# Two heads' pairs of scores ahead and one pair of values behind in three attentions, and four modulation slabs in another place

## The reference

```python
# first block
mod = silu(c) @ w_ada + b_ada                        # "ada1": 6 x 1024 columns
h = rms_norm(x, g1) * (1 + scale1) + shift1
# 8 heads of 64 ("na"): softmax(q k / 8 + bias table) v ; 8 heads of 96 ("mla"): softmax(q k / sqrt(96)) v
merged = sigmoid(gate_na) * (y_na @ w_proj_na) + sigmoid(gate_mla) * (y_mla @ w_proj_mla)
x = x + gate1 * (merged @ w_out)
h2 = rms_norm(x, g2) * (1 + scale2) + shift2         # "the second norm"
x = x + gate2 * (routed_experts(h2) + shared_expert(h2))   # 64 experts, 8 for each token
# second part: two layers; each has its modulation ("ada2": 2 x 3 x 1024 columns)
shift, scale, gate = split(silu(c) @ ada_w[layer] + ada_b[layer])
# layer 0: spatial gating and Fourier mixing on x and on 256 context tokens ("ab")
# layer 1: 16 heads of 64 ("c"), one softmax over [sink, 256 context keys, 256 windowed keys]
out = rms_norm(x, final_g)
```

## Time and profile before

| what | value |
|---|---|
| median of 3 runs | 1321.85 us (1320.67 to 1326.89) |
| the profiled execution | 1322.2 us, its span 1320.4 us |
| TensorE busy | 1255.9 us, 95% of the span |
| VectorE, ScalarE, GpSimd busy | 35%, 25%, 4% |
| mean DMA rate | 251 GB/s over the span |
| mean granted TensorE clock | 0.987 |

### The profile page before, as it was taken

One profiled execution on the slowest core, in us unless ns is written; L12 is line 12 of the kernel. 1 busy time (PEld: TensorE's weight loads), 2 busy tenths in 40 slices (PEclk: granted clock), 3 DMA queues, 4 the chain that ended last, 5 costly groups with the idle time before them and its releaser, 6 DMA issues.

```text
span 1320.4 us, 19746 instructions
## 1 busy us (share of the span) xinstructions
PE 1255.9 (95%) x7605; PEld 776.5 (59%) x7640; DVE 464.1 (35%) x1291; ACT 326.9 (25%) x672; POOL 47.1 (4%) x71
## 2 busy tenths in 40 slices
PE   5999998898899999999999999999999999999886
PEld 3787675587544444444444444446845558888455
DVE  1109594333633333333333333333300112330852
ACT  1213413403222222222222222222211111211761
POOL 0001001111000000000000000000000001000001
PEclk8899999999999999999999999999999999999998
DMA  9936699934399999999999999996121110240000
GB/s 386 345 128 247 267 364 404 376 121 186 125 392 389 387 390 387 388 389 387 388 382 383 383 385 387 389 387 262 64 68 59 64 64 33 96 139 21 1 1 32
DMA packets 47806, 331.61 MB, mean 251 GB/s; under 512 B 5232, under 2 KB 7376, under 8 KB 7824
## 3 DMA queue, kind: packets, MB, share of 16 engines
q1 hardware_dynamic: 44640, 325.08, 62.2%
q10 hardware_dynamic: 2896, 4.19, 0.9%
q0 software_dynamic: 224, 1.70, 0.3%
HBM read 329.90 MB, written 1.05 MB: 251 GB/s over the span
## 4 chain that ended last, share of the span: by engine, by line
PE 91%; ACT 3%; DMA 3%; DVE 2%; issue 1%; SPq 0%; ACTq 0%; DVEq 0%
PE bank L669 18%; PE bank L394 12%; PE bank L693 9%; PE bank L755 8%; PE bank L641 7%; PE bank L649 6%; PE bank L813 4%; PE bank L381 3%; PE bank L317 3%; PE bank L581 2%; PE bank L852 2%; PE bank L567 2%; DMA ring<-stream 2%; PE bank L460 2%; ACT pT L1106 2%; PE bank L371 2%
## 5 line engine op out<-in xcount | busy, mean ns | idle before, releaser
L669 PE MATMUL bank<-ring,arena 128*64 128x512 f32 x1088 | 240.7, 594 | 0.4 <-DMA ring<-experts 0.3
L394 PE MATMUL bank<-hT,ring 128*128 128x256 f32 x736 | 166.1, 386 | 7.2 <-ACT arena L1146 4.1
L394 PEld LDWEIGHTS bank<-hT,ring 128*128 128x128 f32 x736 | 141.7, 194 | 30.9 <-issue 11.3
L669 PEld LDWEIGHTS bank<-ring,arena 128*64 128x64 f32 x1088 | 76.1, 137 | 136.0 <-issue 136.0
L693 PE MATMUL bank<-ring,arena 128*64 128x512 f32 x544 | 124.2, 598 | 0.0
L641 PEld LDWEIGHTS bank<-arena 128*128 128x128 bf16 x1680 | 95.3, 98 | 28.3 <-issue 28.3
L641 PE MATMUL bank<-arena 128*128 128x128 bf16 x1680 | 105.4, 219 | 0.2 <-DVE arena L1630 0.2
L755 PE MATMUL bank<-hT,ring 128*128 128x512 f32 x240 | 104.6, 592 | 0.0
L649 PE MATMUL bank<-arena 128*128 128x512 bf16 x363 | 83.7, 379 | 1.7
L1155 ACT COPY arena<-bank 128x512 f32<-128x512 f32 x70 | 41.0, 586 | 168.6 <-PE bank L641 168.6
L1662 DVE TENSOR_TENSOR arena<-bank,arena 128x512 f32<-128x512 f32 x68 | 43.8, 686 | 105.5 <-ACT arena L1164 105.5
(11 more groups left out here) (296 smaller groups left out, 1349.2 us busy)
## 6 DMA issues: line engine op xcount, KB each, us to landing
ring<-experts SPq DMA_DIRECT2D x204, 1024.0 KB, 7.8
ring<-stream SPq DMA_DIRECT2D x105, 1024.0 KB, 7.0
arena<-consts POOLq DMA_DIRECT2D x1, 1408.0 KB, 7.9
resid<-x SPq DMA_DIRECT2D x1, 1024.0 KB, 6.0
resid<-ctx ACTq DMA_DIRECT2D x1, 1024.0 KB, 5.8
out<-arena ACTq DMA_DIRECT2D x8, 128.0 KB, 2.1
arena<-rpb ACTq DMA_DIRECT2D x2, 438.0 KB, 22.2
cs<-consts ACTq DMA_DIRECT2D x1, 432.5 KB, 9.3
```

Of the source, the lines that this page charges most:

```text
L394: mm = mmul(o[:, 0:n_tok], w[:, k, t * P:(t + 1) * P], hT[:, k, 0:n_tok], start=(k == 0), stop=(k == KT - 1))
L669: mm = mmul(bank[B_GU][64 * u:64 * u + 64, :], xg[:, kk, SLOTS * u:SLOTS * u + SLOTS], w[u][:, k, :], start=(kk == 0), stop=(kk == KT - 1))
```

## The change

Scores run two pairs ahead. "na" and "mla" become one sequence of eight pairs (`EARLY`), so "mla" scores start while "na" still runs. `values` of pair p-1 come after `turn` of pair p. The pairs' scores alternate between banks 0, 1 and 5, 7; outputs have bank 4 alone; in "c" the turned groups go round banks 2, 3 and 5, and the turned probabilities have four buffers (two of them in the arena). The ada2 slabs are split anew: four ahead of the first `turn` (behind `ada_fold(1)`), two with each of the eight pairs, and four in the gap of the second norm, one before its sum and three after. `ada_fold(3)` and `ada(3)` move to the end of "ab", `ada_quarters(3)` behind the router's sigmoid. `pn` no longer waits for "mla"; `wo` waits for `merged` tile by tile; the context's sum takes bank 7, `rtT` bank 4, and `shu` banks 6 and 7.

```diff
+        def turned_at(kind, h):
+            if kind == "c":
+                return pT[:, h % 2, :] if h % 4 < 2 else ar((8192, 13632)[h % 2], 1024)
+            return pT[:, h % 2, 512 * (h % 4 // 2):512 * (h % 4 // 2) + 512]
-        FILL = {(kind, i): [("ada2", 3 * (4 * n + i) + j) for j in range(3)]
-                for n, kind in enumerate(("na", "mla")) for i in range(4)}
+        EARLY = [("na", i) for i in range(4)] + [("mla", i) for i in range(4)]
+        FIRST_FILL = [("ada2", j) for j in range(4)]
+        FILL = [[("ada2", 4 + 2 * p + j) for j in range(2)] for p in range(8)]
+        LAST_FILL = [("ada2", j) for j in range(20, 24)]
...
-                                    open_group(name, h % 2)
+                                    open_group(name, ((0, 1), (5, 7))[i % 2][h % 2])
...
-                        o = open_group(name, 2 + (h % 2 if per == 1 else j))
+                        o = open_group(name, 2 + h % 2 if per == 1 else (2, 3, 5)[(2 * h + j) % 3])
...
-                    o = open_group(name, 4 + i % 2)
+                    o = open_group(name, 4)
...
+            def early_attention():
...
                 scores(0)
+                scores(1)
+                ada_fold(1)
+                for f in FIRST_FILL:
+                    ada_slab(*f)
+                for p, (kind, i) in enumerate(EARLY):
+                    if p + 2 < len(EARLY):
+                        scores(p + 2)
+                    ops[kind][1](2 * i)
+                    ops[kind][1](2 * i + 1)
+                    for f in FILL[p]:
                         ada_slab(*f)
+                    if p >= 1:
+                        values(p - 1)
+                values(7)
+                ada_fold(2)
+
+            def last_attention():
+
+                scores, turn, values = pair_of_heads("c")
+                scores(0)
+                scores(1)
+                for i in range(8):
+                    if i < 6:
+                        scores(i + 2)
                     turn(2 * i)
                     turn(2 * i + 1)
-                    values(i)
+                    if i >= 1:
+                        values(i - 1)
+                values(7)
...
-            pe.wait_ge(S("merged"), 8)
...
+                        if d == 0:
+                            pe.wait_ge(S("merged"), k + 1)
...
+            ada_slab(*LAST_FILL[0])
             two_sums("sq2", "sum2", 0)
+            for f in LAST_FILL[1:]:
+                ada_slab(*f)
...
-            t_tiles("shu", ("shu", 0), 2, [0, 5], 256)
+            t_tiles("shu", ("shu", 0), 2, [6, 7], 256)
...
+            exponents(*EARLY[0])
+            exponents(*EARLY[1])
+            for p in range(8):
+                turned(*EARLY[p])
+                if p < 6:
+                    exponents(*EARLY[p + 2])
+                if p == 3:
+                    ada_quarters(2)
...
+            maxima(0)
+            maxima(1)
+            for p, (kind, i) in enumerate(EARLY):
+                for h in (2 * i, 2 * i + 1):
...
+                    normalise(kind, h, 256)
+                if p >= 2:
+                    rows_out(p - 2)
+                if p + 2 < len(EARLY):
+                    maxima(p + 2)
+                if p == 0:
+                    ada(1)
+            rows_out(6)
+            rows_out(7)
+            ada(2)
...
-            c_scores(0)
-            c_scores(1)
+            for h in range(4):
+                c_scores(h)
             for i in range(8):
...
-                if i < 7:
-                    c_scores(2 * i + 2)
-                    c_scores(2 * i + 3)
-                if i >= 1:
-                    c_out(i - 1)
+                if i >= 2:
+                    c_out(i - 2)
+                if i < 6:
+                    c_scores(2 * i + 4)
+                    c_scores(2 * i + 5)
+            c_out(6)
             c_out(7)
```

More of the change, by code:

```diff
@@ L459, in values, with scores @@
                             hd = head(h)
-                            mm = mmul(o[hd["o"]:hd["o"] + 64, 0:256], hd["v"](kt), pT[:, h % 2, 256 * kt:256 * kt + 256],
+                            mm = mmul(o[hd["o"]:hd["o"] + 64, 0:256], hd["v"](kt), turned_at(kind, h)[:, 256 * kt:256 * kt + 256],
                                       start=(kt == 0), stop=(kt == 2 * per - 1))
                     close_group(mm, name)
-                scores(0)
[L465 to L470, removed]
-                        ada_slab(*f)
+                return scores, turn, values
+            def early_attention():
+                ops = dict(na=pair_of_heads("na"), mla=pair_of_heads("mla"))
+                def scores(p):
+                    kind, i = EARLY[p]
+                    ops[kind][0](i)
+                def values(p):
+                    kind, i = EARLY[p]
+                    ops[kind][2](i)
+                scores(0)
+                scores(1)
[8 more added lines that the diff above has]
+                    for f in FILL[p]:
+                        ada_slab(*f)
+                    if p >= 1:
[9 more added lines that the diff above has]
+                        scores(i + 2)
                     turn(2 * i)
                     turn(2 * i + 1)
-                    values(i)
+                    if i >= 1:
+                        values(i - 1)
+                values(7)
             pe.wait_ge(S("ones_set"), 1)
@@ L552, in _ @@
             pe.wait_ge(S("qk_ready"), 8)
-            attention("na")
-            attention("mla")
-            ada_fold(3)
+            early_attention()
             done(pe, ("na", "o", 3))
-            done(pe, ("mla", "o", 3))
             for half in range(2):
@@ L565, in _ @@
                         o = open_group((tag, d), b + 2 * (d % 2))
+                        if tag == "pm" and d == 0:
+                            done(pe, ("mla", "o", 2))
+                            done(pe, ("mla", "o", 3))
                         for k in range(4):
@@ L798, in _ @@
                     over_chunk(i - 9)
+            ada_fold(3)
             oab = []
@@ L842, in _ @@
                 done(pe, ("v2", t))
-            attention("c")
+            last_attention()
             done(pe, ("c", "o", 7))
@@ L1108, in _, with exponents @@
-            attention("na")
-            attention("mla")
+            def exponents(kind, i):
+                nk = KINDS[kind][2]
+                for h in (2 * i, 2 * i + 1):
+                    act.wait_ge(S(kind + "_negmax"), h + 1)
+                    if kind == "c":
+                        a.activation(att[:, h % 4, 6:8], att[:, h % 4, 2:4], ACT.Exp, bias=vv("sink", h, h + 1))
+                    if kind == "mla":
+                        full(act, ("na", "t", h + 4, 0) if h < 4 else ("mla", "t", h - 4, 0))
+                    for t in range(TT):
+                        o = probs(kind, h)[:, nk * t:nk * t + nk]
+                        src = bk((kind, "s", h))[:, 256 * t:256 * t + 256] if kind == "mla" else o
+                        ins = a.activation(o, src, ACT.Exp, bias=att[:, h % 4, 2 + t:3 + t],
+                                           scale=96 ** -0.5 if kind == "mla" else 1.0,
+                                           accum_out=att[:, h % 4, 4 + t:5 + t])
+                    if kind == "mla":
+                        emptied(ins, (kind, "s", h))
+                    else:
+                        ins.then_inc(S(kind + "_exp"), 1)
@@ new lines, in turned @@
+            def turned(kind, i):
+                for h in (2 * i, 2 * i + 1):
+                    for j in range(KINDS[kind][2] // 256):
+                        full(act, (kind, "t", h, j))
+                        emptied(a.copy(turned_at(kind, h)[:, 512 * j:512 * j + 512], bk((kind, "t", h, j))[:, :]), (kind, "t", h, j))
+            exponents(*EARLY[0])
[6 more added lines that the diff above has]
+                    ada_quarters(2)
@@ L1137, in _ @@
             emptied(a.activation(small[:, 0:128], bk("rt")[:, 0:128], ACT.Sigmoid), "rt")
+            ada_quarters(3)
             second_part(0)
@@ L1247, in _ @@
                     emptied(a.activation(g2s[:, 2 * s + t, :], bk((f"g2{s}", t))[:, 0:256], ACT.Silu), (f"g2{s}", t))
-            attention("c")
+            exponents("c", 0)
+            exponents("c", 1)
+            for i in range(8):
+                turned("c", i)
+                if i < 6:
+                    exponents("c", i + 2)
             load_table(ACT.Sqrt)
```

72 lines of the change are left out of this document (16 added, 56 removed).

## The result

The changed kernel takes 1303.76 us (median of 4, 1302.35 to 1304.08) against 1323.88 us for the kernel before on the same chip (1320.67 to 1326.89): a ratio of 0.9834, 95% interval 0.9813 to 0.9854, so it is faster, by 1.7%. The forecast was 1302.4 us. The profiled execution took 1303.9 us with a span of 1302.1 us, 18.3 us less than the one before. The medians are 20.1 us apart, since the executions of the kernel before lie in two groups (1320.7 and 1321.9 us, 1325.9 and 1326.9 us) and the profiled one belongs to the first. It is the pair of profiled executions that the table divides.

What follows compares the result with a forecast made beforehand. TensorE, 91% of the chain, was taken as the bound. Gains of 9.8 - 0.5 + 1.4 + 0.4 + 3.4 + 4.9 = 19.4 us off 1322.2, less 0.35 for the median, gave 1302.4 us; range 1297.5 to 1307.

Steps and rivals of the forecast that it cites:

- Forecast 9.8: First attentions: the fold after them ends at 246.2 us against the merge's start at 256.03, a gain of 9.8 us.
- The pause before the first fold: First attentions: TensorE stands about 3.4 us for bank 7 until VectorE has added head 3's bias.
- rival (1): Clock falls in the pause before the first fold: 1.8 us, 1304.2; with a second fall around `pos` 1306; chance 0.22.
- the sum of TensorE's own work: First attentions from 202.9 us: turnings, slabs, `values`, scores and one bank wait add to 42.7 us, ending at 245.6.
- rival (2): DMA bounds the first attentions; if all four slabs' gain of 3.7 us were lost, 1306.1 us; chance 0.05.
- one of the signs I had named for a wrong prediction: Gap before the router: the prediction is wrong if the router starts later after the norm because of the three slabs.
- The term that I had put at 3.4: Shared expert: with banks 6 and 7 VectorE reads `pos` at 343.9 instead of 347.34 us; bounds 2.0 and 4.1.
- the allowance of 0.33 us in each of seven pairs: Last attention: small waits traded between TensorE and VectorE move its end from 1273.5 to 1275.8 us; gain 4.9.
- Rival (3): VectorE holds the last attention at nearly 7 us a pair; that part gives 1.7 us, total 1305.6; chance 0.10.
- rival (4): Slower: transposes behind the next pair's maxima lengthen each of 16 pairs; 1.3 us each eats the gain; chance 0.02.
- the other sign that I had named for a wrong prediction: Expert stage: it only shifts as a whole; the prediction is wrong if the experts take more than their 550 us.
- The case that was forecast, clock unharmed: Whole kernel: all gains come and TensorE keeps full clock, 1302.4 us; chance 0.58.

Runs made afterwards that it cites:

- e9: As e5, but VectorE copies a pair's outputs out at the head of the next pair's work: 1309.7 us, ratio 0.9889 to the kernel before.
- e3: The changed kernel with the four slabs of the second norm's gap taken back into the first attentions: 1305.91 us, ratio 0.9851 to the kernel before.
- e2: The changed kernel with the first fold behind the four first slabs instead of ahead of them: 1296.64 us, ratio 0.9776 to the kernel before.
- e8: The changed kernel with four products that nothing reads put on TensorE ahead of `pos`: 1301.35 us, ratio 0.9818 to the kernel before.
- e12: The changed kernel with e2's edit, `pos` in bank 5 and four products without a use behind `pos`: 1295.83 us, ratio 0.9766 to the kernel before.
- e4: The changed kernel with the shared expert's second tile group (`shu`) back in banks 0 and 5: 1306.56 us, ratio 0.9857 to the kernel before.
- e11: The changed kernel with scores, exponents and maxima one pair ahead in the last attention, banks unchanged: 1308.02 us, ratio 0.988 to the kernel before.
- e5: The changed kernel with `values` right behind the same pair's `turn` in the first attentions: 1323.78 us, ratio 0.9986 to the kernel before.
- e10: The changed kernel with first-attention scores, maxima and exponents one pair ahead, plus e2's edit: 1300.34 us, ratio 0.9813 to the kernel before.

## Why the prediction was right, and where it was not

**First attentions.** Forecast 9.8, measured 10.4, out of terms that missed in both directions. The pause before the first fold came, 3.69 us (forecast 3.4), released by VectorE, as worked out from the bias of heads 2 and 3. The step that failed is that the clock would outlast it: rival (1) was the case, price 1.4 us. What offset it is the sum of TensorE's own work, and that it did so is luck. For scores and turnings I had added row lengths; starts of neighbouring rows lie closer. A pair of "mla" takes 5.68 us from turning to turning, where my terms (2.29, 1.09, 1.86, 1.01) make 6.25. "mla" scores advance 1.83 us now. Even from start to start they took 2.22 us before (233.26 to 235.48 us); I put that down to bank waits inside them, each too short for a bracket. Over four pairs this is 4 x 0.46 = 1.8 us, and the eight turnings take 8.3 instead of 8.7 us, some 2.3 us in all. The waits before `values` went (e9: 5.8 us longer with them), the four slabs were worth 3.5 (e3, forecast 3.7), the last wait for bank 4 was 0.53 (forecast 0.7). DMA, rival (2), is out: no slab was waited for, not even at 420 GB/s in e2.

**Merge to router.** 1.6 against 1.4; no experiment takes this part back, so it rests on the rows alone. The four slabs cost 0.2 us instead of nothing, by which the router does start later after the norm, one of the signs I had named for a wrong prediction. The rest of the router's wait is 1.42 us (forecast 1.3), and its matmuls run at full clock (granted clock 1.00 from 308 to 312 us).

**Shared expert.** VectorE reads `pos` 3.6 us earlier after the router, as forecast (3.4). But behind it stands the second fall of the clock. TensorE's timeline, then VectorE's, of the changed kernel:

```profile
308.12 3.35 PE L636 MATMUL bank<-hT,wr 128*64 128x256 f32 x16 [1.42 <-ACT hT L1060]
...
313.61 13.98 PE L402 MATMUL bank<-hT,ring 128*128 128x256 f32 x64
329.84 0.41 PE L659 MATMUL bank<-pT,cs 128*128 128x64 f32 x2 [2.26 <-DVE arena L1664]
...
332.49 1.48 PE L679 MATMUL bank<-arena 128*128 128x512 bf16 x3 [1.27 <-DVE pT L1672]
333.77 4.75 PE L686 MATMUL bank<-arena 128*128 128x128 bf16 x48
...
339.31 1.08 PE L714 MATMUL bank<-ring,arena 128*64 128x512 f32 x4
```

```profile
329.01 0.69 DVE L1664 TENSOR_TENSOR arena<-bank,arena 128x256 f32<-128x256 f32 x2
...
331.33 0.23 DVE L1671 COPY pr<-bank 128x64 f32<-128x64 f32 x1 [0.84 <-PE bank L663]
```

TensorE was so much earlier that it stood 2.26 us for bank 7 and 1.27 us for the gates. From VectorE's read to the first expert matmul it is 5.64 us before, in e8 (331.30 to 336.94) and in e12 (325.47 to 331.11), all at full clock there, and 7.98 us here: 2.3 us of slow clock. The term that I had put at 3.4, with a lower bound of 2.0 for just this case, is 3.6 - 2.3 = 1.2 us net, outside its bounds. e4 shows that the pause and its price were there before too, only earlier in the chain.

**Last attention.** The mechanism was right; the mis-sized term is the allowance of 0.33 us in each of seven pairs for engines that trade waits, 2.3 us. From the first transposes to the end of the last `values` the sum without it is 44.0 us and the trace has 45.4, so 1.4 us was due; and the first transposes come 0.4 us sooner after the first scores than I had them. TensorE in "c":

```profile
1228.76 1.99 PE L454 MATMUL bank<-cs,arena 128*128 128x128 f32 x16
1230.67 1.95 PE L468 MATMUL bank<-arena 128*64 128x256 f32 x16
1232.55 1.99 PE L444 MATMUL bank<-arena 64*128 64x512 f32 x8
1234.47 2.26 PE L454 MATMUL bank<-cs,arena 128*128 128x128 f32 x16
...
1252.00 2.28 PE L454 MATMUL bank<-cs,arena 128*128 128x128 f32 x16 [1.69 <-DVE arena L1445]
```

A pair takes 5.7 to 6.0 us (forecast 6.1 to 6.4). From 1222.75 us there is no bracket until 1252 us, when TensorE has no more scores to make and waits once, 1.69 us, for VectorE. Ahead of that it loses at most 0.3 us in a turning row (2.26 against 1.99 us). So two engines at nearly the same pace with room between them pay mostly once near the end: 6.2 instead of 4.9. Rival (3), 7 us a pair, and rival (4), slower, are out; 6.53 us in e11 is what comes without the second pair ahead.

**Experts.** The stage took 1.1 us more, against "shifts as a whole", the other sign that I had named for a wrong prediction. TensorE's waits for expert slabs are 1.3 us in the page after and 0.3 us in the one before. Over the experiments with the same code there the stage took 550.3 us (waits 0.2) to 553.2 us (waits 2.2), so I count it as the run's own.

So the number held because of offsets: two falls of the clock (3.7 us) and the experts (1.1) against TensorE's work taken too long (some 2.3 in the first attentions) and "c" (1.3). The case that was forecast, clock unharmed, was not the case that ran; it was rival (1) in both places, which I had at 1306 us, and that the 1303.8 us measured lie closer to the forecast is luck.

## What to carry to other kernels

When work is taken out of a pause, or an order made tighter, look for the first instruction that now stands longer, and put independent work ahead of it: one line moved (e2) brought 5 us more in its stage. How far ahead scores are made pays only where the softmax engines are at the pace of TensorE ("c"), not where they have slack ("na", "mla"); there the step that pays is to put other work between a copy and its use, and that needs its output bank read out in time (e5 against e9). For the sum over a pipelined stage take start to start, not row lengths, and don't charge each pair a wait where engines of equal pace have room between them. And before a difference of two profiles is put down to an edit, see whether it lies in a stage that the edit touches: here 2 of e2's 7 us and 1.4 of e9's 7.15 us did not come from the edit.

## What the hardware showed

Pauses shorter than the 4.1 us ones of before were followed by work at 1.2 GHz: 3.69 us at the first fold (price 1.4 in the changed kernel), 2.26 and 1.27 us with little between them at `pos` (2.3), 1.76 us in e10 (1.5), three of the four 2.25 us pauses in e5. The Trainium skill (TensorE: Matmul & The Clock Gate, "A second HAM failure mode: psum-queue depth-cycling") says that even short pauses between groups of matmuls can make the clock go back and forth between its levels. By that, e5 with its pause in each pair would run part of its stage at the lower level, and the trace agrees: 0.88 on the mean.

The length of the pause alone doesn't decide it. The 3.37 us pause of e5 passed without a fall (granted clock 1.00 from 212 to 222 us), and so did the third of the four 2.25 us pauses there, 1.70 us in the kernel before and 1.69 us in "c" of the changed kernel, while the same wait in e10 was followed by 1.6 us of loss.

Nor is the price fixed. Behind the same 3.69 us pause the same four slabs took 5.08 to 6.47 us in nine profiles, against 3.66 us at full clock, a price of 1.4 to 2.8 us. From the router to the first expert matmul the same code took 29.8 to 31.2 us in ten profiles, against 28.75 us in e8. What decides it no run here shows, and a price of the clock from one profile is known to no better than about 1 us.

Whole executions of one kernel differ by the clock too. Of ten of the kernel before, taken beside e12, one took 1321.5 us at a mean clock of 0.988, nine 1326.6 to 1328.2 us at 0.982 to 0.985. No profile shows one of the nine, so which stretch makes the difference is open.
